# Gate-and-up products of a feed-forward layer: three seven-product units in a chunk instead of two

## What is computed

```python
D_MODEL = 2048; SEQ = 256; D_FF = 5632

def _swiglu_ffn(x, norm_g, w_gate, w_up, w_down):
    h = _rmsnorm(x, norm_g)
    return (jax.nn.silu(h @ w_gate) * (h @ w_up)) @ w_down

h = h + 0.5 * _swiglu_ffn(h, ffn1_norm[l], ffn1_w_gate[l], ffn1_w_up[l], ffn1_w_down[l])
...
h = h + 0.5 * _swiglu_ffn(h, ffn2_norm[l], ffn2_w_gate[l], ffn2_w_up[l], ffn2_w_down[l])
return _rmsnorm(h, final_norm)
```

## Time and profile before

| | us |
|---|---|
| median of three runs | 2593.12 |
| lowest and highest | 2592.7, 2596.25 |
| the profiled execution | 2596.25 |
| its span | 2594.5 |
| TensorE busy in it | 2562.4 (99%) |
| VectorE busy | 1955.1 (75%) |
| ScalarE busy | 1340.6 (52%) |
| GpSimd busy | 188.7 (7%) |

### The profile page before, as it was taken

The page is one execution under the profiler, slowest core; times in us unless marked ns, Lnnn a source line. Parts: engine busy times, 40 slices in busy tenths (PEclk is TensorE's granted clock), DMA queues, the critical chain, the costliest instruction groups (busy, mean ns, idle before and its releaser), DMA issues.

```text
span 2594.5 us, 34224 instructions
## 1 busy us (share of the span) xinstructions
PE 2562.4 (99%) x13659; PEld 2105.0 (81%) x13659; DVE 1955.1 (75%) x2311; ACT 1340.6 (52%) x1568; POOL 188.7 (7%) x346
## 2 busy tenths in 40 slices
PE   8999999999999999999999999999999999999998
PEld 7888888888888777878788888888888888887887
DVE  6888888887767796959666766555668888888876
ACT  5555555555556466446455544433455555555554
POOL 2000000000000011010001112000100000000000
PEclk9999999999999999999999999999999999999999
DMA  6767676667676575556488879643767776776665
GB/s 213 229 211 239 213 237 212 220 207 228 217 210 195 184 229 158 179 164 179 147 280 255 251 242 285 202 155 130 236 190 232 224 226 223 227 223 226 202 196 175
DMA packets 278576, 548.21 MB, mean 211 GB/s; under 512 B 25020, under 2 KB 35424, under 8 KB 278032
## 3 DMA queue, kind: packets, MB, share of 16 engines
q1 hardware_dynamic: 253904, 478.60, 58.3%
q0 software_dynamic: 24192, 66.89, 8.7%
q10 hardware_dynamic: 320, 0.53, 0.1%
HBM read 508.15 MB, written 37.77 MB: 210 GB/s over the span
## 4 chain that ended last, share of the span: by engine, by line
PE 85%; DVE 8%; issue 3%; ACT 2%; DMA 1%; POOL 0%; SPq 0%; DVEq 0%; ACTq 0%; POOLq 0%
PE pp L794 14%; PE pp L796 14%; PE pp L795 14%; PE pp L415 11%; PE pp L417 10%; PE pp L416 10%; DVE wlo L376 2%; PE pa L794 1%; PE pa L796 1%; PE pa L795 1%; PE pb L796 1%; PE pb L794 1%; PE pb L795 1%; ACT whi L371 1%; PE pa L2402 1%
## 5 line engine op out<-in xcount | busy, mean ns | idle before, releaser
L376 DVE TENSOR_TENSOR wlo<-raw,whi 128x1024 fp32r<-128x1024 f32 (+1 forms) x764 | 919.5, 1216 | 352.5 <-ACT whi L371 332.9
L371 ACT ACTIVATE whi<-raw 128x1024 fp32r<-128x1024 f32 (+1 forms) x764 | 798.4, 1054 | 623.5 <-PE pp L417 431.9
L796 PE MATMUL pp<-wlo,xhi 128*128 128x512 f32 x1040 | 405.1, 389 | 0.0
L794 PE MATMUL pp<-whi,xhi 128*128 128x512 f32 x1040 | 405.1, 389 | 0.0
L795 PE MATMUL pp<-whi,xlo 128*128 128x512 f32 x1040 | 405.0, 389 | 0.0
L415 PE MATMUL pp<-whi,xhi 128*128 128x512 f32 (+1 forms) x928 | 371.2, 400 | 0.7 <-DVE xlo L533 0.7
L417 PE MATMUL pp<-wlo,xhi 128*128 128x512 f32 (+1 forms) x928 | 360.3, 388 | 0.0
L416 PE MATMUL pp<-whi,xlo 128*128 128x512 f32 (+1 forms) x928 | 360.1, 388 | 0.0
L847 ACT ACTIVATE whi<-tw 128x1024 fp32r<-128x1024 f32 x124 | 131.6, 1062 | 276.3 <-PE pp L796 124.3
L794 PEld LDWEIGHTS pp<-whi,xhi 128*128 128x128 f32 x1040 | 195.3, 188 | 40.5
L796 PEld LDWEIGHTS pp<-wlo,xhi 128*128 128x128 f32 x1040 | 195.3, 188 | 40.5
(11 more groups left out here) (528 smaller groups left out, 3671.0 us busy)
## 6 DMA issues: line engine op xcount, KB each, us to landing
raw<-in_ffn_w_gate SPq DMA_DIRECT2D x176, 512.0 KB, 4.3
raw<-in_ffn_w_up SPq DMA_DIRECT2D x176, 512.0 KB, 4.7
raw<-in_ffn_w_down SPq DMA_DIRECT2D x176, 512.0 KB, 4.6
raw<-in_w_in SPq DMA_DIRECT2D x144, 512.0 KB, 4.3
hid_dram<-hid_t POOLq DMA_DIRECT2D x43, 512.0 KB, 5.0
xq<-hid_dram POOLq DMA_DIRECT2D x156, 128.0 KB, 3.6
raw<-in_w_lift SPq DMA_DIRECT2D x32, 512.0 KB, 6.2
raw<-in_w_out SPq DMA_DIRECT2D x32, 512.0 KB, 5.0
```

The lines of the kernel that those rows point to most:

```text
L371: nc.scalar.activation(whi[:, s, :, 0:width], raw[:, r % RING, :, 0:width], ACT.Copy).then_inc(whi_ready, 1)
L376: nc.vector.tensor_tensor(wlo[:, s, :, 0:width], raw[:, r % RING, :, 0:width], whi[:, s, :, 0:width].bitcast(F32), ALU.subtract).then_inc( ...
L794: nc.tensor.matmul(out, a_hi, whi[:, s, block, :], start=start, stop=False)
L796: return nc.tensor.matmul(out, a_hi, wlo[:, s, block, :], start=False, stop=stop)
```

## The change

Chunks 1 to 9 do row group 5 as a unit too: three units behind t = 1, 3 and 5 of ten plain slots. Chunk 10 keeps two units. The forms of row group 5 are made in chunk 0 from the high and low part of the input (`whole_five`), and lie where the hidden part of chunk 9 comes later, which is why chunk 10 has none. `copy_first`, `combine` and `combine_last` stay at the same distance behind the last unit; as there are only ten slots now, the low part of the hidden chunk (`hidden_lo`) follows the add of the gate at once, at t = 9, where t = 10 and 11 stood between them.

```diff
@@ -122,7 +122,8 @@
 
 
 SEVEN = range(1, NFC)
-GU_UNITS, GU_AFTER = (6, 7), (1, 5)
+GU_UNITS = {i: (5, 6, 7) if i < NFC - 1 else (6, 7) for i in SEVEN}
+GU_AFTER = {i: (1, 3, 5) if i < NFC - 1 else (1, 5) for i in SEVEN}
 DN_UNITS = {"f1": ((0, 1, 2, 3, 4, 5), (2, 3, 4, 5)), "f2": ((0, 1, 2, 3, 4, 5), (0, 1, 2, 3, 4, 5))}
 DN_AFTER = {"f1": ((5, 9, 13, 17, 21, 25), (5, 9, 13, 17)), "f2": ((5, 9, 13, 17, 21, 25), (1, 5, 9, 13, 17, 21))}
 DN_FORMS = {3: 0, 7: 1, 15: 2}
@@ -202,7 +203,7 @@
     def ffn(tag):
         turned(tag + "norm", NDC, nat=False, by_pe=NDC if tag == "f1" else 1)
         turned(tag + "act", NFC, by_pe=0)
-        products(tag + "gu", 2 * NFC, [KT], ups=nats[tag + "act"], seven=lambda i: (GU_UNITS, GU_AFTER) if i in SEVEN else None)
+        products(tag + "gu", 2 * NFC, [KT], ups=nats[tag + "act"], seven=lambda i: (GU_UNITS[i], GU_AFTER[i]) if i in SEVEN else None)
         products(tag + "dn", NDC, [FT], seven=lambda q: (DN_UNITS[tag][q], DN_AFTER[tag][q]))
 
     ffn("f1")
@@ -231,11 +232,11 @@
 
     sums, acts, banks = [], [], []
     for tag in ("f1", "f2"):
-        sums.append((tag, "x"))
-        acts.append((tag, "x"))
-        banks.append((tag, "x"))
+        sums += [(tag, "x5"), (tag, "x")]
+        acts += [(tag, "x5"), (tag, "x")]
+        banks += [(tag, "x5"), (tag, "x")]
         for i in SEVEN:
-            for u in GU_UNITS:
+            for u in GU_UNITS[i]:
                 sums += [(tag, "gu", i, u, step) for step in (1, 2, 3)]
             acts += [(tag, "gu", i, "copied"), (tag, "gu", i, "gate")]
             banks.append((tag, "gu", i))
@@ -298,6 +299,9 @@
         xs_dn = at("xs_dn", 215, [2, 4, P])
         xshi = at("xshi", 215, [2, 4, P], F32R)
         xslo = at("xslo", AR + 40, [2, 4, P], F32R)
+        xs_five = at("xs_five", 211, [1, 4, P])
+        whole_five = at("whole_five", 213, [2, T])
+        five = [at("fivehi", AR + 36, [1, 4, P], F32R), at("fivelo", AR + 38, [1, 4, P], F32R)]
         cb = at("cb", AR + 80, [4, CW])
         hs_f1 = [at("hshi_f1", 68, [6, 4, P], F32R), at("hslo_f1", 84, [6, 4, P], F32R)]
         hs_f2 = [at("hshi_f2", 72, [6, 4, P], F32R), at("hslo_f2", 84, [6, 4, P], F32R)]
@@ -919,11 +923,12 @@
                 wait_pair(pe, pair["a"]["free"])
                 for t in range(len(pair["plain"])):
                     plain_pe(pe, pair, t, (xhi, xlo))
-                    if t in GU_AFTER:
-                        n = GU_AFTER.index(t)
+                    if t in pair["after"]:
+                        n = pair["after"].index(t)
                         if n == 0:
                             pe.wait_ge(sem("banks_free"), BANKS[tag, "x"] if i == SEVEN[0] else BANKS[tag, "gu", i - 1])
-                        unit_pe(pe, pair, n, (xhi, xlo), (xshi, xslo), n)
+                        j = pair["units"][n][0]
+                        unit_pe(pe, pair, n, (xhi, xlo), five if j == 5 else (xshi, xslo), 0 if j == 5 else j - 6)
             pe.wait_ge(x_ready, s0 + NFC - 1)
             for q in range(NDC // 2):
                 pair, after = dn[2 * q]["pair"], DN_AFTER[tag][q]
@@ -962,6 +967,8 @@
                     act.wait_ge(slot_used, gu[0]["done"])
                     act.wait_ge(nat_ready, n0)
                     scaled_silu(act, gs, gu[0]["par"]).then_inc(sem(gu[0]["released"][0]), 1)
+                if j == 5:
+                    forms_hi(act, xs_five[:, :, :, :], five[0][:, :, :, :], (tag, "x5"))
                 if j == 6:
                     forms_hi(act, xs_gu[:, :, :, :], xshi[:, :, :, :], (tag, "x"))
             for i in SEVEN:
@@ -969,9 +976,9 @@
                 gate = pair["a"]
                 for t, (_, _, w, _) in enumerate(pair["plain"]):
                     split_hi(act, w, 0)
-                    if t in GU_AFTER:
-                        unit_act(act, pair, GU_AFTER.index(t), (tag, "gu", i))
-                    if t == pair["na"]:
+                    if t in pair["after"]:
+                        unit_act(act, pair, pair["after"].index(t), (tag, "gu", i))
+                    if t == pair["after"][-1] + 1:
                         act.wait_ge(nat_ready, n0 + i)
                         copy_first(act, pair, cb[:, 0, :])
                     if t == pair["na"] + 3:
@@ -1042,7 +1049,13 @@
                 if j == 3 and tag == "f1":
                     norm_recip(dve, 0)
                 if j == 4:
+                    dve.wait_ge(x_ready, turns[tag + "norm"][1] + NDC)
+                    link(dve, v.tensor_tensor(whole_five[:, :, :], xhi[:, 10:12, :].bitcast(F32), xlo[:, 10:12, :].bitcast(F32), ALU.add))
+                    forms(dve, whole_five, xs_five, (tag, "x5"))
+                if j == 5:
                     forms(dve, xf, xs_gu, (tag, "x"))
+                if j == 6:
+                    forms_lo(dve, xs_five[:, :, :, :], five[0][:, :, :, :], five[1][:, :, :, :], (tag, "x5"))
             forms_lo(dve, xs_gu[:, :, :, :], xshi[:, :, :, :], xslo[:, :, :, :], (tag, "x"))
             for i in SEVEN:
                 pair = gu[2 * i]["pair"]
@@ -1051,17 +1064,17 @@
                     split_lo(dve, w, 0)
                     if t == 3:
                         nat_turn(dve, None, nats[tag + "act"] + i - 1)
-                    if t in GU_AFTER:
-                        n = GU_AFTER.index(t)
+                    if t in pair["after"]:
+                        n = pair["after"].index(t)
                         if n == 0 and i == SEVEN[0]:
                             dve.wait_ge(sem("banks_free"), BANKS[tag, "x"])
                         unit_dve(dve, pair, n, (tag, "gu", i), between=(lambda: gated(i - 1)) if n == 0 else None)
-                    if t == pair["na"] + 2:
+                    if t == pair["after"][-1] + 3:
                         combine(dve, pair, cb, (tag, "gu", i))
-                    if t == pair["na"] + 3:
+                    if t == pair["after"][-1] + 4:
                         combine_last(dve, cb, (tag, "gu", i))
                         v.tensor_tensor(cb[:, 0:2, :], pair_of(gate), cb[:, 0:2, :], ALU.add).then_inc(sem(gate["released"][0]), 1)
-                    if t == pair["na"] + 5:
+                    if t == len(pair["plain"]) - 1:
                         dve.wait_ge(sem("acts_ready"), ACTS[tag, "gu", i, "gate"])
                         hidden_lo(dve, tag, i - 1, hhi[:, 4 * i - 4:4 * i, :], hlo[:, 4 * i - 4:4 * i, :])
             for q in range(NDC // 2):
```

## The result

The changed kernel takes 2681.55 us (median of four runs, 2673.37 to 2682.9), the kernel before on the same occasion 2594.68 us. The ratio is 1.032, with a 95% interval of 1.030 to 1.034. The median is 87 us longer, where 77 were forecast. The profiled execution of the change took 2673.37 us, its span is 2671.6 us.

The account below looks back on a forecast made before the run. TensorE bounds the kernel before; with three units VectorE would, at 46.7 us a chunk against 42.2. Nine chunks less 3.7 plus 1.8 us give 38.6 us per layer, 77 in all: 2670 us, range 2628 to 2706.

Parts of the forecast that it names:

- The bound: Gate-and-up chunks: TensorE sets the pace before; with three units VectorE needs 43.9 us without load waits, TensorE 41.5 us.
- The walk through the list: VectorE's instructions in one three-unit chunk, timed from slot 0's split: third unit starts at 27.7, chunk ends at 46.7 us.
- The tail of 19.0 us: VectorE from the start of a chunk's last unit to the split of the next chunk's slot 0: 18.97 us.
- the 0.7 us that the walk puts down to slot 8: Wait for slot 8's load in the rows used for the tail; without it VectorE's chunk is 43.2 us.
- The loads: Third unit's second weight load, disturbed by reads of the hidden part: 6.3 us; chunk 46.7 us, bounds 45.1 and 48.5.
- The second unit: Between first and second unit VectorE has 5.4 us of work, loads land after 5.1 us: nothing lost.
- The edges: Per layer, VectorE's lead absorbs 3.7 us of the loss once; chunk 10, entered without it, is charged 1.8 us.
- The sum: Per layer 9 x (46.7 - 42.2) - 3.7 + 1.8 = 38.6 us, two layers 77 us: profiled execution 2673, median 2670 us.
- The signs: Chunks 2 to 9: VectorE over 85% busy, TensorE waiting for low parts, longest VectorE idle ahead of third unit, then silu.
- sign of being wrong: TensorE busy without a gap in these chunks, or the third unit's load landed when VectorE comes to it.
- The other side: Rival: VectorE keeps up, TensorE never stands, each unit saves three matmuls: 2581 us; chance 0.05.
- The clock: Rival: short gaps put TensorE on its 1.2 GHz level for one unit per chunk, 86 us more, some 2756 us; chance 0.02.

Follow-up runs that it names:

- the gating cut: Gating of chunks 1 to 9 cut to 8 of 512 columns: in the change 2643.74 us, in the kernel before 2597.76 us against 2597.62.
- The light reads: The change with reads of the turned hidden part cut to 128 B per row instead of 4 KB in chunks 2 to 10: 2654.36 us.
- the run again: The unaltered change measured a second time, on another chip beside the kernel before: 2682.27 us, ratio 1.033.
- the gaps filled: The change with silu in the next chunk, combining ahead of slot 8, hidden split at t = 5, third weight sum early: 2600.19 us, ratio 1.0009.

## Why the prediction was right

- **The bound.** That VectorE takes over from TensorE in chunks with three units is shown by the gating cut in both kernels (38 us and nothing) and by TensorE's full windows in chunks with two.
- **The walk through the list.** In the chunk shown each of its stations was met within 0.3 us. The tail of 19.0 us, made of rows of the second unit of the kernel before, measures 19.02 us (223.93 to 242.95). That it fits is in part luck: the 0.7 us that the walk puts down to slot 8 do not stand there in chunk 10, where VectorE idles for 0.17 us ahead of it; those rows have about as much in small idle times elsewhere, and in the change slot 8 waits for 0.7 to 1.9 us.
- **The loads.** Taken at 6.3 us for the second load; 6.2 us in the chunk shown and 6.1 us as the mean of 18, from 4.9 to 8.0 us, with waits from 1.4 to 4.5 us. The light reads show both parts of the term.
- **The second unit** had no wait in the sum. It has 0.16 to 1.06 us in three of nine chunks of the first layer, a small term that was missing.
- **The edges.** The sum had 81 us for 18 chunks, less 3.8 us for the edges of the two layers. By the windows the 18 chunks took 78.9 us more than before (36.4 and 42.5), and the whole profiled execution 77.1 us more, so everything outside them gave back 1.8 us. Which of the edge's two terms (3.7 us of lead, 1.8 us in chunk 10) was off is open.
- **The sum.** 2673 us for the profiled execution was forecast, and it took 2673.37. That it fits so closely is luck: 2 us too much for the chunks met 2 us too much given back at the edges, and the profiled execution was the fastest of its four. The forecast for the median was 2670 us, and the medians (2681.55, 2682.27) are 12 us above it. Of these, 2 to 3 us are the kernel before, slower on the later occasions (2594.68 and 2596.5 for 2593.12). Loads that land later are a part of the rest: the profiled execution of the run again took 2677.26 us, 3.9 us more than that of the change, and VectorE waited for loads for 54.5 us in it, 4.5 us more (lines below). The other executions have no trace, so what made them longer is not shown.
- **The signs.** VectorE is busy for 85.7% and 84.6% of the nine chunks in the two layers, where over 85% was named. TensorE waits at slot 0 of each chunk and in the first and third units, but only now and then in the second. Each chunk's idle time of VectorE is on average longest ahead of the third unit and next ahead of the hidden low part. Neither sign of being wrong came.
- **The other side** would have needed VectorE idle for less than 1.2 us in a chunk. Even with the gaps filled it was 2.7 us (24 us in nine chunks).
- **The clock** stayed at 1.00, the level of 2.4 GHz, in all the stretches shown, with TensorE's waits of 0.2 to 2.1 us in them.

VectorE's waits for loads, first in the change at 1984 to 2401 us (the first layer stands above), then in the run again at 73 to 490 and 1984 to 2406 us:

```profile
DVE tw L876 <- DMA raw<-in_ffn_w_up: 27.6, 13, 4.5
```

```profile
DVE tw L876 <- DMA raw<-in_ffn_w_up: 25.9, 12, 3.9
DVE tw L876 <- DMA raw<-in_ffn_w_up: 28.6, 10, 4.9
```

## What to carry to other kernels

Saving matmuls with extra elementwise sums only pays while the engine that makes the sums has room for them and for its fixed waits; walk its list once from end to end, with the starts of the trace, before trusting its busy share. In a ring, ask which instruction frees the buffer that the next load needs, and count from there to the landing. Idle time in a list can be filled by work that has no hurry, and that was worth some 75 us here, but a load that then starts half a microsecond later may land in other traffic.

## What the runs showed of the hardware that was not expected

- Two loads of 512 KB issued 0.2 us ahead of four reads of 128 KB each from the other queue landed after 3.9 and 6.2 us; issued 0.5 us behind them in another order of the list, after 4.9 and 7.6 us. Over the 18 chunks of the change the second load took 4.9 to 8.0 us. With the reads cut to a thirty-second, the wait for them was nearly constant (1.1 to 1.6 us in chunks 2 to 9 of the first layer, 1.1 to 1.9 us in the second), so most of the scatter of this kernel's chunks comes from that meeting.
- TensorE's granted clock was 0.998 on average in the changed kernel, with waits of 0.2 to 2.1 us ahead of its matmuls in every chunk with three units, and 0.999 in the kernel before.
